# A third norm squared by halves, a second single-use place for a load, and no constant products ahead of the first norm

## What is computed

```
# first block
h = x + rms_norm(merged(rms_norm(x) @ w_in ...) @ w_out)        # norm 1, branches, merge
h = h + rms_norm((silu(gate) * up) @ w_ffn_out)                  # norm 2, feed-forward
h = h + sigmoid(h @ w_ple_gate) * (p @ w_ple)                    # gated embedding
# second block
a = modulate(rms_norm(h, g_mix), shift, scale)                   # norm 3
qkv = a @ w_in_2 ; two kinds of attention over 8 heads each      # dilated (qd, kd, vd), stick-breaking (qs, ks, vs)
h = h + gate * (mixed @ w_out_2)
y = moe(modulate(rms_norm(h), ...))                              # 32 experts, 2 per token, of 1024 x 512 x 1024
out = rms_norm(h + gate_ffn * y)                                 # final norm

rms_norm(x, g) = x * rsqrt(mean(x * x) + 1e-6) * g
```

## Time and profile before

| | |
|---|---|
| median of 3 runs | 1133.38 us |
| lowest, highest | 1132.96, 1134.09 us |
| the profiled execution | 1130.97 us, its span 1128.9 us |
| PE busy | 1033.6 us, 92% of the span |
| PEld, DVE, ACT, POOL busy | 792.3, 508.8, 376.9, 494.0 us |
| mean granted clock of PE | 0.981 |
| DMA | 342.16 MB, mean 303 GB/s |
| expert loads | 192 of 1024 KB |

### The profile page before, as it was taken

The page is one execution under the profiler, slowest core; times in us unless marked ns, Lnnn a source line. Parts: engine busy times, 40 slices in busy tenths (PEclk is TensorE's granted clock), DMA queues, the critical chain, the costliest instruction groups (busy, mean ns, idle before and its releaser), DMA issues.

```text
span 1128.9 us, 19763 instructions
## 1 busy us (share of the span) xinstructions
PE 1033.6 (92%) x8510; PEld 792.3 (70%) x8510; DVE 508.8 (45%) x905; ACT 376.9 (33%) x537; POOL 494.0 (44%) x209
## 2 busy tenths in 40 slices
PE   8999999999999999998999998989978888888676
PEld 7989999999799999887998894444443433434232
DVE  2998977565357668123345553133121211212113
ACT  6355544643563444455675431000000000000002
POOL 6886899867686788986665410000000000000000
PEclk9999999999999999999999999999998999989899
DMA  9555455456479898756344689999999999999994
GB/s 366 202 184 179 159 181 179 163 207 250 168 258 340 324 365 332 301 186 266 116 151 172 273 353 395 421 420 419 421 420 421 420 421 420 420 421 420 421 419 169
DMA packets 48330, 342.16 MB, mean 303 GB/s; under 512 B 5361, under 2 KB 5745, under 8 KB 7410
## 3 DMA queue, kind: packets, MB, share of 16 engines
q1 hardware_dynamic: 46944, 337.56, 75.6%
q10 hardware_dynamic: 1298, 3.32, 0.8%
HBM read 339.81 MB, written 1.05 MB: 302 GB/s over the span
## 4 chain that ended last, share of the span: by engine, by line
PE 57%; DMA 27%; POOL 5%; DVE 4%; ACT 3%; SPq 2%; issue 1%; DVEq 0%; ACTq 0%
DMA ring<-in_gu 15%; PE ps L492 13%; PE ps L494 13%; PE ps L493 13%; PE ps L1083 5%; POOL spl L2316 5%; DMA raw<-in_stream 5%; PE ps L1130 4%; DMA ar<-in_gu 3%; DMA ar<-in_dn 2%; DMA ring<-in_dn 2%; PE ps L1119 2%; PE ps L1063 2%; SPq L2387 2%; ACT sph L1185 1%
## 5 line engine op out<-in xcount | busy, mean ns | idle before, releaser
L2316 POOL TENSOR_TENSOR spl<-raw,sph 128x1024 fp32r<-128x1024 f32 x204 | 493.6, 2453 | 157.8 <-ACT sph L1185 157.8
L1185 ACT ACTIVATE sph<-raw 128x1024 fp32r<-128x1024 f32 x204 | 205.8, 1053 | 141.6 <-DMA raw<-in_stream 91.0
L492 PE MATMUL ps<-xbh,sph 128*128 128x256 f32 x608 | 172.9, 284 | 3.7 <-DVE xbl L1682 1.7
L493 PE MATMUL ps<-xbl,sph 128*128 128x256 f32 x608 | 172.0, 283 | 0.0
L494 PE MATMUL ps<-xbh,spl 128*128 128x256 f32 x608 | 172.0, 283 | 0.0
L492 PE MATMUL ps<-xah,sph 128*128 128x256 f32 x576 | 165.0, 286 | 2.0 <-DVE xal L1682 1.7
L493 PE MATMUL ps<-xal,sph 128*128 128x256 f32 x576 | 163.0, 283 | 0.0
L494 PE MATMUL ps<-xah,spl 128*128 128x256 f32 x576 | 162.9, 283 | 0.0
L2250 DVE TENSOR_TENSOR ar<-ar,ps 64x256 f32<-64x256 f32 x32 | 13.5, 423 | 266.3 <-ACT ar L1620 266.3
L1620 ACT ACTIVATE ar<-ps 64x256 f32<-64x256 f32 x32 | 12.1, 378 | 340.1 <-PE ps L1083 340.1
L1130 PE MATMUL ps<-ar,ar 128*128 128x512 f32 x256 | 125.0, 633 | 0.0
(11 more groups left out here) (300 smaller groups left out, 1365.6 us busy)
## 6 DMA issues: line engine op xcount, KB each, us to landing
raw<-in_stream SPq DMA_DIRECT2D x127, 1024.0 KB, 4.9
ring<-in_gu SPq DMA_DIRECT2D x115, 1024.0 KB, 26.9
ring<-in_dn SPq DMA_DIRECT2D x57, 1024.0 KB, 27.5
ar<-in_gu SPq DMA_DIRECT2D x7, 1024.0 KB, 26.4
slotx<-in_gu SPq DMA_DIRECT2D x6, 1024.0 KB, 26.9
ar<-in_dn SPq DMA_DIRECT2D x4, 1024.0 KB, 27.1
slotx<-in_dn SPq DMA_DIRECT2D x3, 1024.0 KB, 26.2
X<-in_x SPq DMA_DIRECT2D x2, 512.0 KB, 4.9
```

Of the source, the lines that this page charges most:

```text
L492: e.matmul(o, sh, mh, start=start, stop=False)
L493: e.matmul(o, sh, ml, start=False, stop=False)
L1185: e.activation(u.half(SPH[u.n % NSP], h), u.half(RAW[u.slot], h), ACTF.Copy).then_inc(w.up(hi_ok), 1)
L2316: e.tensor_tensor(u.half(SPLO[u.n % NSP], h), u.half(RAW[u.slot], h), u.half(SPH[u.n % NSP], h), ALU.subtract).then_inc(w.up(lo_ok), 1)
```

## The change

Three edits, and what they need of room:

- The third norm: ACT squares halves of 512 channels (`half_square`). Both first halves (q = 0 and q = 2) are squared ahead of the third sigmoid, the second half of tile 0 behind the last sigmoid, that of tile 1 behind tile 0's root. DVE turns the sums of the first halves into a bias, sum/1024 + eps, once for both tiles, and the root reads the sum of the second half with that bias (`half_root`). The dummy root is gone. On DVE the copy of the old x stands behind both reciprocals. `TMPA` moves, because the embedding that it overlaid is still read.
- The expert stream: s = 3 also gets a single-use place, in the arena at 6144, where the values' transposed scores lie until the second product `dv_mm` 2. The ring is as large as before; its order moves by one for s from 5 on. `HN`, `SWT`, `HS` and one `XG` change places, `GFI` follows.
- The eight constant products and the memset of `FILL` are taken out.

```diff
-        FILL = ar(10480, 384)
-        TMPA = at("tmpa", O_XA, 1024)
+        TMPA = at("tmpa", O_XA + 3072, 1024)
-        HN = ar(6144, 2048, 2)
+        HN = ar(1024, 2048, 2)
-        ONCE = 4
-        SLOT.append(ar(8192, 2048))
+        ONCE = {3: NS, 4: NS + 1}
+        SLOT += [ar(6144, 2048), ar(8192, 2048)]
-            return NS if s == ONCE else (s - (s > ONCE)) % NS
+            return ONCE.get(s, (s - (2 if s > 4 else 0)) % NS)
-        SWT = [ar(1024 + 256 * n, 256) for n in range(2)]
-        HS = [ar(1536 + 256 * n, 256) for n in range(2)]
+        SWT = [ar(6144 + 256 * n, 256) for n in range(2)]
+        HS = [ar(6656 + 256 * n, 256) for n in range(2)]
-        XG = [k8(ar(2048, 1024)), k8(at("xg1", (const_at["dist"][0] + 7) // 8 * 8, 1024))]
-        GFI = ar(2048, 1024)
+        o_xg = (const_at["dist"][0] + 7) // 8 * 8
+        XG = [k8(at("xg0", o_xg, 1024)), k8(ar(7168, 1024))]
+        GFI = at("gfi", o_xg, 1024)
-        slot_sem.append(d_wr)
+        slot_sem += [d_gfp, d_wr]
...
# tensor, ahead of the first norm
-            w.wait_ge(blank_ok, 2)
-            for _ in range(8):
-                e.matmul(ps[7][:, 0:256], FILL[:, 0:128], FILL[:, 128:384], start=True, stop=True)
...
# scalar
+            def half_square(tt, half):
+
+                w.wait_ge(x_ok, x3(2 * tt + half))
+                own()
+                e.activation(TMPA[:, 512 * half:512 * half + 512], X[:, tt, 512 * half:512 * half + 512], ACTF.Square,
+                             accum_out=ss6[:, 2 * tt + half:2 * tt + half + 1]).then_inc(w.up(nsq_ok), 1)
+
+            def half_root(tt):
+
+                w.wait_ge(rv_ok, 5)
+                own()
+                e.activation(ss3[:, tt:tt + 1], ss6[:, 2 * tt + 1:2 * tt + 2], ACTF.Sqrt, bias=sse3[:, tt:tt + 1],
+                             scale=1.0 / D).then_inc(w.up(nsq_ok), 1)
...
             take(first["ple_gate"] + 2)
+            half_square(0, 0)
+            half_square(1, 0)
             gate(1)
             take(first["ple_gate"] + 3)
-            norm_square(ss3, TMPA, 0, x3(1))
             gate(3)
+            half_square(0, 1)
...
-            warm(ACTF.Sqrt)
-            norm_root(2, ss3, 0, DG)
-            norm_square(ss3, TMPA, 1, x3(3))
-            norm_root(2, ss3, 1, DG)
+            half_root(0)
+            half_square(1, 1)
+            diagonal(2, 0, ss3, DG, 6)
+            half_root(1)
+            diagonal(2, 1, ss3, DG, 7)
...
# vector
-            e.memset(FILL, 1.0).then_inc(w.up(blank_ok), 1)
...
             gated_embedding(0)
             gated_embedding(2)
+            w.wait_ge(nsq_ok, 10)
+            own()
+            e.tensor_scalar(sse3, ss6.rearrange("p (t h) -> p t h", t=2)[:, :, 0], 1.0 / D, EPS, ALU.mult, ALU.add)\
+                .then_inc(w.up(rv_ok), 1)
             gated_embedding(1)
             gated_embedding(3)
-            inverse(2, 0, ss3)
+            w.wait_ge(nsq_ok, 12)
+            invert(ss3[:, 0:1], rv_ok)
+            w.wait_ge(nsq_ok, 14)
+            invert(ss3[:, 1:2], rv_ok)
             old(0)
-            inverse(2, 1, ss3)
...
# sync, the loop over s
                 if s == 2:
                     w.wait_ge(dt_mm, 8)
-                elif s == ONCE:
-                    w.wait_ge(dv_mm, 1)
-                elif s == 5:
+                elif s == 3:
+                    w.wait_ge(dv_mm, 2)
+                elif s == 6:
                     raws_free(0, 1)
...
-                elif s == 20:
+                elif s == 21:
                     w.wait_ge(y0_mm, 1)
```

More of the change, by code:

```diff
@@ L357, in program @@
         ss1, ss2, ss3 = small(2), small(2), small(2)
+        ss6, sse3 = small(4), small(2)
         st, mv, nb = small(24), small(4), small(2)
@@ L449, in head @@
             return QK[kind][64 * (h % 2):64 * (h % 2) + 64, h // 2, :]
-        slot_landed, per_slot = {}, [0] * (NS - NRAW) + [16 * sum(u.slot == i for u in units) for i in range(NRAW)] + [16]
+        slot_landed, per_slot = {}, [0] * (NS - NRAW) + [16 * sum(u.slot == i for u in units) for i in range(NRAW)] + [16, 16]
         for s, entry in enumerate(EXPERT_WEIGHTS):
@@ L1171, in warm @@
             def warm(func):
-                w.wait_ge(blank_ok, 2)
+                w.wait_ge(blank_ok, 1)
                 w.wait_ge(warm_ok, w.n(warm_ok))
@@ L1199, in root, with diagonal @@
                 return e.activation(ss, ss, ACTF.Sqrt, bias=c_("eps"), scale=scale)
-            def diagonal(n, tt, ss, dg):
-                w.wait_ge(rv_ok, 2 * n + tt + 1)
+            def diagonal(n, tt, ss, dg, inverted=None):
+                w.wait_ge(rv_ok, inverted or 2 * n + tt + 1)
                 e.activation(dg[:, 128 * tt:128 * tt + 128], ident, ACTF.Copy, scale=ss[:, tt:tt + 1])\
@@ L2364, in sync @@
                     w.wait_ge(dt_mm, 8)
-                elif s == ONCE:
-                    w.wait_ge(dv_mm, 1)
-                elif s == 5:
+                elif s == 3:
+                    w.wait_ge(dv_mm, 2)
+                elif s == 6:
                     raws_free(0, 1)
-                elif s == 7:
+                elif s == 8:
                     w.wait_ge(half_used, 2 * units[first["vs"] + 1].n + 2)
-                elif s == 9:
+                elif s == 10:
                     w.wait_ge(sv_mm, 2)
-                elif s == 10:
+                elif s == 11:
                     raws_free(2)
-                elif s == 11:
+                elif s == 12:
                     raws_free(3)
-                elif 12 <= s < 20:
-                    w.wait_ge(half_used, 2 * w_out_units[min((s - 10) // 2, 3)].n + 2)
-                elif s == 20:
+                elif 13 <= s < 21:
+                    w.wait_ge(half_used, 2 * w_out_units[min((s - 11) // 2, 3)].n + 2)
+                elif s == 21:
                     w.wait_ge(y0_mm, 1)
```

## The result

| | before | after |
|---|---|---|
| median of 10 runs each | 1132.12 us | 1126.39 us |
| profiled execution, its span | 1130.97, 1128.9 us | 1125.90, 1124.1 us |
| last instruction ends | 1122.91 us | 1121.10 us |
| from there to the span's end | 6.0 us | 3.0 us |
| first weight product | 13.29 us | 13.95 us |

The ratio is 0.9948, interval 0.9932 to 0.9963: 5.7 to 5.9 us faster, where the forecast was 2.3.

What follows compares the result with a forecast made beforehand. TensorE was taken to set the pace up to about 678 us, the DMA engines from there. Expert load -2.50, third norm -0.10 and start +0.30 gave -2.30 us off the 1133.38 median: 1131.1 us, range 1129.8 to 1132.8.

Steps and rivals of the forecast that it cites:

- The slot edit: Expert stream: a second single-use place puts the loads one ahead; -2.50 us, ends -2.6 and 0.
- The issues at 618.9: SP queue: loads s = 3, 4 and 5 leave from 618.5 us on, three issues near there.
- the filled stretch: DMA between 624 and 631 us, at 14 GB/s before: the additional load falls into this empty time.
- the unbroken stream: Expert loads after 678.41 us: three issued loads cover the gap of some 1.7 us, so engines stay busy.
- Rival C: Expert stream after 678 us: engines run dry again and the load's lead is lost; 1133.6 us, chance 0.10.
- The start: First norm without constant products: TensorE begins at half rate, first weight product later; +0.3 us, bounds 0 and +1.0.
- rival D: Start: clock stays low beyond the norm into the first weight products, until 21 us; 1134.4 us, chance 0.07.
- The third norm: Squares by halves bring the second diagonal 1.2 us earlier, worth -0.1 us; bounds -0.6 and +0.3.
- tile 0's products start at 532.55, 0.26 later, tile 1 directly behind: Third norm on TensorE: tile 0 ends at 534.41, where tile 1 starts instead of at 534.49.
- the copy of the old x: Third norm on DVE: moved behind both reciprocals, it ends near 534.6 us, ahead of the first scaling.
- Rival E: Third norm: the table switch in front of a true root costs 1.3 us more; 1132.5 us, chance 0.07.
- A: Whole kernel, the forecast itself: 1131.1 us, its own range 1130.3 to 1132.0; chance 0.64.

Runs made afterwards that it cites:

- e17: The changed kernel run again, unaltered, in a later sitting; 1128.31 us, ratio 0.9944.
- e10: The changed kernel with four constant products of 240 columns ahead of the third norm; 1127.19 us, ratio 0.9950.
- e2: The kernel before with the third norm's edit (squares by halves) alone; 1132.92 us, ratio 1.0008.
- e4: The changed kernel with the eight constant products at the start put back; 1130.08 us, ratio 0.9982.
- e5: The changed kernel with eight one-column products added at expert 20; 1131.25 us, ratio 0.9990.
- e3: The kernel before without the eight constant products at the start and their memset, alone; 1128.47 us, ratio 0.9966.
- e6: The kernel before with 32 one-column products added at expert 20; 1131.72 us, ratio 0.9991.
- e9: The kernel before with the second single-use place and without the eight constant products at the start; 1128.38 us, ratio 0.9951.
- e11: The kernel before with four constant products of 512 columns at the start instead of eight of 256; 1129.04 us, ratio 0.9965.
- e14: The kernel before with 56 one-column products added at expert 20; 1129.87 us, ratio 0.9965.
- e15: The kernel before with 64 one-column products added at expert 20; 1132.58 us, ratio 0.9995.
- e1: The kernel before with the second single-use place alone and the moved buffers it needs; 1130.46 us, ratio 0.9985.
- e13: The kernel before with 44 one-column products added at expert 20; 1126.98 us, one run only.
- e16: The changed kernel with eight constant products ahead of the third norm and 56 one-column products at expert 20; 1126.62 us, ratio 0.9940.
- e7: The changed kernel with eight constant products of 240 columns ahead of the third norm's products; 1129.49 us, ratio 0.9970.
- e8: The changed kernel with start products put back, eight constant products ahead of the third norm and 24 one-column ones at expert 20; 1129.32 us, ratio 0.9972.
- e12: The kernel before with the slot edit, no start products, four constant products ahead of the third norm; 1126.41 us, ratio 0.9943.
- e18: Kernel before with slot edit, no start products, four constant products ahead of third norm, run again in a later sitting; 1126.61 us, ratio 0.9930.

## Why the prediction was wrong

**The slot edit: right.** The issues at 618.9, the filled stretch, the unbroken stream. Sized -2.50; the profiles give -2.2 to -2.55 (442.29 and 441.95 against 444.50 us), the medians 1.7 to 2.8. The last load lands at 1106.43 instead of 1108.25 us, although the restart at 678.81 is 0.4 later. Rival C's second break didn't come.

**The start: right in kind, twice the size in this execution.** Taken +0.30, bounds 0 to +1.0; measured +0.66 here and +0.59 in e17. Over all profiles the first weight product comes at 13.02 to 13.95 us in the ten kernels without the products at the start (mean 13.54) and at 12.92 to 13.29 in the ten with them (mean 13.10), so the term is some +0.4. The forecast took the half rate to last 3.2 us, as in its row; in the profile of after the loads stood 0.21 us apart until 12.9 us, 5.7 us from the first, and the 32 took 6.35 us (5.08 in e10). Weight products are spaced as before from 14 us on, so rival D's low clock beyond the norm didn't happen. The Trainium skill ("TensorE: Matmul & The Clock Gate", Part 1) says that the instant of the clock's rise differs between runs of one kernel. The two profiles of the changed kernel agree: the loads of the first norm went from 0.21 us apart to 0.12 at 12.9 us in one and at 11.4 us in the other (e17).

**The third norm: the step "tile 0's products start at 532.55, 0.26 later, tile 1 directly behind" was taken at the clock of before's row.** The first half of it was right: 4.65 us from gate to tile 0 against 4.45, so 0.20 later. Two things were missed. First, the clock: the changed kernel fell to 0.84, and TensorE's one idle stretch of 3.62 us stands ahead of it. With the norm edit and no eight gap products all six profiles fell (after, e2, e4, e5, e10, e17). But the norm of before, idle for 3.42 us, fell as well in six profiles (e3, e6, e9, e11, e14, e15) and stood in three (before, e1, e13). The full clock in before's row was the rarer draw and not a property to build on; whether the edit itself worsens the odds, nine profiles against six don't settle. Second, a wait that the forecast judged only against DVE's first scaling: the copy of the old x, moved behind both reciprocals, also frees a bank that TensorE needs. At full clock it makes TensorE wait 0.35 us in the middle of tile 0 (e16's row above), which eats the 0.34 that was gained between the tiles. At full clock the edit thus costs 0.2 us (10.91 in e7, e8 and e16 against 10.70 in e1, e12, e13 and e18) where -0.1 was forecast; in the profile of after, with the clock, the term is +1.4. Rival E's drain didn't come: root at 530.02, load from 528.73 for 1.28. The drain of some 1.38 us that the Trainium skill names ("ScalarE: Activation LUTs", What ACT_TABLE_LOAD costs) is thus not seen in front of a true root either; the measurement decides.

**What failed is the sum: a term was missing.** "The profiled execution took 1130.97 (span 1128.9 and 2.1 around it)": the forecast carried everything behind the last load over as a constant, and looked at the constant products only where they run. Taking them out had no term at the end of the program. The span held 6.0 us behind the last instruction, 3.2 of them a wait of SyncE for TensorE's sequencer, and it stood in the list of SyncE's waits. With 32 TensorE instructions fewer 3.0 us of it were gone, and TensorE's branch at the end took 0.37 us in place of 3.73. By the experiments: 3.7 us for the products alone (e3, with a later first product), 3.7 for halving their number at the same work (e11), about 3 between e14 and e15. The forecast's other terms add up to -2.30, with the end's -3.0 to -5.3, which is inside what was measured (5.7 to 5.9, interval 4.2 to 7.7). The forecast's 1131.1 us missed by 4.7 us, of which another 1.3 are its base: before's median was 1133.38 us over three runs and 1132.12 over ten.

Two slips in the forecast's sums changed nothing: by the bounds that it names, A's own range begins at 1130.5 us and not at 1130.3, and E comes to 1132.4 and not 1132.5.

**What is left.** From the first product to the gate the profile of after was 1.68 us shorter (512.87 against 514.55 us). No edit touches this stretch. The changed kernel took 515.50 there in its second profile, and the other kernels, e9 apart, 512.65 to 515.35: it is scatter between executions, and here it hid the third norm's +1.4. The 0.0002 to 0.0014 by which sums of parts and whole differ are below what these runs tell.

## What to carry to other kernels

Look at what stands between the last counted instruction and the end of the span, at the waits of the engines for each other's sequencers there, and at how long each engine's last branch takes: an edit that only changes how many instructions an engine has can be worth more than one that moves work (3 us here). Test it with products that do nothing, at two lengths, before crediting an edit with it; and since it comes and goes with the length, tune it last. Where a forecast rests on a full clock behind an idle stretch of TensorE, price both levels: here the same code and the same 3.42 us of idling gave 10.70 us at one and 11.58 to 12.90 at the other.

## What the runs showed of the hardware

- SyncE's last wait for TensorE's sequencer was 2.6 to 3.5 us or 0.2, never between, in 20 profiles. Which of the two it was went with TensorE's instruction count, in a manner that fits a period of 256.
- The wait was there where TensorE's branch at the end took 2.98 to 4.06 us, with a 16,384-byte packet of instructions starting during it (nine profiles), and not where the branch took 0.37 to 0.48 us without one (eleven).
- Products that nobody reads cost nothing that shows at an expert that waits for data: 64 of them left the median at 1132.58 us against 1132.81, and with 56 of them (224 instructions) the kernel was 2.9 us faster.
- Behind an idle stretch of 3.42 us TensorE's granted clock in 528:539 was 1.00, 0.84 or 0.69 in kernels with the same norm; eight constant products in the stretch (0.51 us of idling ahead of the norm) kept it at 1.00 three times out of three, four kept it with the old norm twice and not with the new one.
